# Attention in a hybrid block: the value pieces' remainders on VectorE, and seven products of the second row block ahead of the last value products

## The chip, the core and the metric

The kernel runs on one core of a Trainium2 chip. TensorE multiplies matrices into PSUM, which has 8 banks of 128 x 512 f32. VectorE (DVE in the profile), ScalarE (ACT) and GpSimd (POOL) do the rest, and SyncE (SP) issues most transfers. Each engine runs its own program in order, and the programs are tied together by semaphores: `then_inc` raises one, `wait_ge` holds an engine until it has reached a value. The metric is the time of one execution on the device in microseconds (us), median over several runs.

## The reference, cut to what matters

A block with two branches over 1024 tokens and 1024 channels: a gated delta rule and, beside it, sparse attention over latent keys and values with 8 heads of 128. Both are projected, gated and merged:

```python
ckv = rms_norm(ckv, kv_norm_g[l])
q_lat = jnp.einsum('bthd,chd->bthc', qb, w_uk[l]) * DSA_DH ** -0.5
o_lat = dsa_attention(q_lat, ckv, qi, ki, wi, rel_bias)    # softmax over the chosen keys, times the values
ob = jnp.einsum('bthc,chd->bthd', o_lat, w_uv[l]).reshape(B, T, DSA_W) * jax.nn.silu(zb)
yb = ob @ w_o_dsa[l]
out = (ga * ya + gb * yb) @ w_out[l]
x = x + gate[:, None] * out
return rms_norm(x, final_g)
```

In the kernel's words: the keys and values of each head are the latents times `w_uk` and `w_uv` ("pieces"); logits, softmax and value products follow for each head; the result `ob` times `w_o_dsa` is the projection of the merge; it is gated by `gb` and added to the half `m1` that the other branch has left in memory; and the sum `m` times `w_out` is the output. Every product is made of three f16 or bf16 products of high and low parts (`three`), so that it comes near f32.

## The kernel before, in words

Three stages stand one after the other on TensorE, each written out by hand: the delta rule, attention (`phase_attention`) and merge (`phase_merge`). The change is in attention and in the first lines of the merge.

**Attention.** There are 64 steps n, 8 for each head, in the order of tiles `ORDER = (0, 7, 1, 6, 2, 5, 3, 4)`: the step of tile i has i + 1 blocks of 128 keys. Two steps make a pair q (32 pairs), and every engine walks over the pairs.

- TensorE in pair q: `logits` of the steps 2q and 2q + 1, then `values` of the pair q - 3, then one `piece` (a half of the keys or of the values of the next head: 6 products of 512 columns or 24 of 128), then one `cut`.
- VectorE in pair q: `norm` (a reciprocal) of the pair before, two `peak` (logits plus bias, and their maximum), `gate` of pair q - 4, and `low` twice (the low part of the probabilities of the pair before).
- ScalarE in pair q: `high` twice (the high part of the probabilities of the pair before), `soften` twice (the exponentials), `piece` (the high part of the piece, out of PSUM), and `rest`.
- SyncE turns each step's probabilities with a DMA transpose (L2433) once `high` and `low` are done. `values` waits for it.
- GpSimd splits the gated result of a pair into high and low parts and raises `b_l` (L2677).

A piece m is number j = m % 4 of its head: j = 0 and 1 are keys, 2 and 3 are values. Its low part (its remainder) is what is left when the high part is taken away. For the pieces 4 to 31, TensorE does that in PSUM with one more product of 512 columns, by minus the identity (`cut`, L2482 for keys, L2484 for values), and ScalarE then copies the remainder out (`rest`, L2558 and L2560). For the pieces 0 to 3, VectorE subtracts (L2598, L2601). Pieces stand in the banks 5 and 7 by turns, and each is read by the engines one pair after it was made.

**The end of attention.** When the logits are through (pairs 32 to 34), `begin_projection` puts 4, 5 and 5 products of the merge's first two blocks (`project_rows`, three matmuls of 512 columns each) ahead of the value products of the last three pairs.

**The merge.** `project_blocks` makes 16 blocks of 8 products (k = 0 to 7). Of the first four, two have had their first seven products in `begin_projection`, one gets them at the head of `project_blocks`, ahead of the wait for `b_l` at 32, and the fourth (b, half) = (1, 1) makes all eight behind it. SyncE starts the merge's loads only when attention is over, and so do the others (`attention_left`):

```python
def attention_left(engine):
    engine.wait_ge(g.b_l, NT * H // 2)
    engine.wait_ge(g.pv, NT * H // 2)
```

In this order SyncE then loads two parts of `w_out` (L2192), two tiles of x, two rows spread over all partitions, and the first tile of `gb` (`channel_gates`, L2204). VectorE treats the 16 blocks n in order: L2298 multiplies block n by its `gb`, L2301 adds `m1`, ScalarE makes the high part `m_hi` (L2270), and L2304 makes the low part and raises `lo_ok`. GpSimd meanwhile splits six parts of weights (L2235 and L2237); the third raises `w_ready` to 3, for which TensorE waits ahead of block 8. The output products of the first tile take up k in order, and each k waits for two more low parts:

```python
if i == 0 and c0 == 0:
    pe.wait_ge(lo_ok, 2 * k + 1)
```

So k = 7 waits for the fifteenth L2304.

## Time and profile before

| | |
|---|---|
| median of 3 runs | 1370.96 us (1369.11 to 1371.2) |
| profiled execution, its own time | 1369.57 us |
| its span, first to last instruction | 1367.8 us |
| TensorE busy | 1334.2 us, 98% |
| VectorE busy | 912.9 us, 67% |
| ScalarE busy | 718.5 us, 53% |
| GpSimd busy | 593.7 us, 43% |
| attention on TensorE | about 1046 to 1202.9 us |
| the merge's projection on TensorE | 1202.9 to 1276.7 us |
| output products | 1276.7 to 1359.8 us |

The shares are averages over the whole span. TensorE's weight loads (PEld) run beside its matmuls. A matmul's duration reaches from its start to its last result, so that matmuls overlap: what one of them costs is read from the distance of two starts. Times in the trace count from the start of the span.

### The profile page before, as it was taken

How to read it: one execution, taken by the hardware profiler on the slowest of the kernel's cores; microseconds unless marked ns; L12 is line 12 of the kernel's file. 1: busy time of each engine (PE TensorE's matmuls, PEld its weight loads, DVE VectorE, ACT ScalarE, POOL GpSimd, SP SyncE). 2: the span in 40 equal slices, each digit the busy share in tenths (PEclk: the TensorE clock that was granted, in tenths of full speed). 3: DMA queues.
4: the chain of work that ended last, by engine and by line, in shares of the span. 5: the costliest groups of instructions: out<-in, count | busy, mean ns of one | idle time of the engine just before them, and what ended most of it. 6: DMA issues, size and time to landing. Idle time of an engine off the chain costs nothing.

```text
span 1367.8 us, 26191 instructions
## 1 busy us (share of the span) xinstructions
PE 1334.2 (98%) x9966; PEld 803.1 (59%) x9974; DVE 912.9 (67%) x1857; ACT 718.5 (53%) x1490; POOL 593.7 (43%) x653
## 2 busy tenths in 40 slices
PE   6899999999999999999999999999999999999997
PEld 6456994444444456666666666655445777644444
DVE  4889787777432577688788786545733788737544
ACT  4768777786443645556656645333123888701111
POOL 0074677878772434424434423002121688765000
PEclk9999999999999999999999999999999999999999
DMA  9401333333324222323233233335875988985222
GB/s 367 154 9 32 110 95 115 124 109 124 115 71 140 75 79 63 89 64 77 70 98 79 75 98 101 110 104 162 301 253 170 150 162 163 163 275 173 82 92 93
DMA packets 230056, 170.55 MB, mean 125 GB/s; under 512 B 109122, under 2 KB 202154, under 8 KB 228268
## 3 DMA queue, kind: packets, MB, share of 16 engines
q1 hardware_dynamic: 229084, 164.39, 42.7%
q10 hardware_dynamic: 720, 4.46, 0.8%
q8 instruction: 79, 1.29, 0.4%
q14 instruction: 45, 0.37, 0.1%
q0 software_dynamic: 128, 0.03, 0.0%
HBM read 114.40 MB, written 31.15 MB: 106 GB/s over the span
## 4 chain that ended last, share of the span: by engine, by line
PE 54%; POOL 4%; DVE 3%; DMA 3%; issue 2%; ACT 1%; SPq 1%; DVEq 0%; POOLq 0%; ACTq 0%
PE ps L94 15%; PE ps L96 14%; PE ps L95 14%; POOL g_shared L1434 2%; POOL g_shared L1432 1%; DVE g_yq L1674 1%; DMA g_shared<-diagonal_blocks 1%; PE ps L2065 1%; PE ps L1954 1%; DMA g_o<-g_piece 1%; PE ps L2049 1%; PE ps L2044 1%; PE ps L2048 1%; SPq L1321 1%; PE ps L2064 1%
## 5 line engine op out<-in xcount | busy, mean ns | idle before, releaser
L94 PE MATMUL ps<-g_h_hi,g_piece_hi 128*128 128x512 f16 x544 | 207.1, 381 | 1.6 <-PEq L2717 1.6
L95 PE MATMUL ps<-g_h_lo,g_piece_hi 128*128 128x512 f16 x544 | 206.5, 380 | 0.0
L96 PE MATMUL ps<-g_h_hi,g_piece_lo 128*128 128x512 f16 x544 | 206.5, 380 | 0.0
L1432 POOL TENSOR_TENSOR g_shared<-g_shared 128x120 f32<-128x120 f32 (+14 forms) x120 | 56.2, 468 | 174.5 <-DMA g_shared<-diagonal_blocks 164.2
L1042 DVE TENSOR_SCALAR_CACHE_REDUCE a_ada<-a_ada,a_s_all 128x896 bf16<-128x896 f32 (+1 forms) x124 | 113.0, 967 | 1.0
L1674 DVE SCALAR_TENSOR_TENSOR g_yq<-e_raw,g_taps,g_yq 128x1024 f32<-128x1024 f32 x60 | 96.4, 1606 | 22.1 <-ACT g_yq L1496 20.1
L94 PE MATMUL ps<-g_o,g_h_hi 128*128 128x128 f16 (+2 forms) x424 | 100.2, 267 | 3.4 <-DMA g_o<-g_piece 2.7
L96 PE MATMUL ps<-g_o,g_h_lo 128*128 128x128 f16 (+2 forms) x424 | 100.1, 267 | 0.4
L95 PE MATMUL ps<-g_o,g_h_hi 128*128 128x128 f16 (+2 forms) x416 | 97.1, 265 | 0.0
L96 PEld LDWEIGHTS ps<-g_h_hi,g_piece_lo 128*128 128x128 bf16 x544 | 53.2, 98 | 64.3 <-issue 0.2
L94 PEld LDWEIGHTS ps<-g_h_hi,g_piece_hi 128*128 128x128 f16 x544 | 53.3, 98 | 54.4 <-issue 2.0
L95 PEld LDWEIGHTS ps<-g_h_lo,g_piece_hi 128*128 128x128 f16 x544 | 53.3, 98 | 51.3
L1528 ACT ACTIVATE g_shared<-ps,e_s_neg 128x128 f32<-128x128 f32 x56 | 20.6, 367 | 100.4 <-PE ps L2049 100.1
L1434 POOL TENSOR_TENSOR g_shared<-g_shared 128x120 f32<-128x120 f32 (+14 forms) x120 | 59.9, 499 | 9.4
L310 POOL TENSOR_TENSOR a_work<-a_w,a_work 128x512 bf16<-128x512 f32 x48 | 56.5, 1193 | 15.3 <-ACT a_work L738 15.3
L310 POOL TENSOR_TENSOR a_parts<-a_w,a_parts 128x512 bf16<-128x512 f32 x48 | 55.0, 1159 | 13.3 <-ACT a_parts L738 13.3
L1665 DVE TENSOR_TENSOR g_piece_lo<-g_piece,g_piece_hi 128x1024 bf16<-128x1024 f32 x32 | 40.3, 1260 | 27.0 <-ACT g_piece_hi L1583 24.2
L755 ACT ACTIVATE a_ada<-a_ada,a_s_all 128x1024 bf16<-128x1024 f32 (+1 forms) x62 | 57.3, 927 | 0.7 <-DVEq L1064 0.7
L94 PEld LDWEIGHTS ps<-g_o,g_h_hi 128*128 128x128 f16 x424 | 41.4, 98 | 20.7 <-DMA g_o<-g_piece 3.4
L2270 ACT ACTIVATE g_h_hi<-g_arena 128x512 f32 x16 | 10.1, 630 | 80.1 <-DVE g_arena L2301 80.1
L95 PEld LDWEIGHTS ps<-g_o,g_h_hi 128*128 128x128 f16 x424 | 41.5, 98 | 16.1
L2565 ACT ACTIVATE g_o<-g_o,l_top 128x128 f32<-128x128 f32 (+3 forms) x64 | 49.0, 768 | 2.5 <-DVE l_top L2611 2.5
(450 smaller groups left out, 3983.2 us busy)
## 6 DMA issues: line engine op xcount, KB each, us to landing
a_w<-in_w_in SPq DMA_DIRECT2D x17, 1024.0 KB, 6.1
g_piece<-in_w_in SPq DMA_DIRECT2D x34, 512.0 KB, 4.2
channel_gates<-a_ada SPq DMA_DIRECT2D x48, 256.0 KB, 2.2
g_shared<-diagonal_blocks SPq DMA_DIRECT2D x32, 256.0 KB
a_ada<-in_w_ada ACTq DMA_DIRECT2D x4, 1024.0 KB, 9.8
a_x<-in_x SPq DMA_DIRECT2D x8, 512.0 KB, 9.1
delta_gate<-a_ada SPq DMA_DIRECT2D x16, 256.0 KB, 2.6
g_shared<-sums_by_head SPq DMA_DIRECT2D x8, 512.0 KB, 4.1
```

Of the source, the lines that this page charges most:

```text
L94: pe.matmul(out, a_hi, b_hi, start=first, stop=False)
L95: pe.matmul(out, a_hi, b_lo, start=False, stop=False)
L96: return pe.matmul(out, a_lo, b_hi, start=False, stop=last)
L310: nc.gpsimd.tensor_tensor(op_lo[v % 2][:, x], of, op_hi[v % 2][:, x], ALU.subtract).then_inc(w_ready, 1)
L755: nc.scalar.activation(mask[:, g.first[i]:g.first[i + 1]], score[:, g.first[i]:g.first[i + 1]], ACT.Sign, bias=trial[:, 4 + e:5 + e], accu ...
L1042: mark(("count", e), nc.vector.tensor_scalar(spent_of(i), rows_of(i), trial[:, e:e + 1], offset[:, e:e + 1], ALU.is_ge, ALU.add, accum_out ...
L1432: nc.gpsimd.tensor_tensor(part, table[:, j, :, j + 1:BASE], tc[:, :, j:j + 1].broadcast_to([P, NT, left]), ALU.mult).then_inc(sub, 1)
L1434: last = nc.gpsimd.tensor_tensor(tc[:, :, j + 1:BASE], tc[:, :, j + 1:BASE], part, ALU.subtract)
L1528: nc.scalar.activation(n_sb[:, c], at(6 + c, 1), ACT.Copy, scale=(s_neg if i else s_pos)[:, i, h:h + 1]).then_inc(n_ok[c], 1)
L1665: nc.vector.tensor_tensor(w_lo[:, m % 3], w32[:], w_hi[:, m % 3], ALU.subtract).then_inc(w_ready, 1)
L1674: nc.vector.scalar_tensor_tensor(out=y, in0=raw[:, m % 2, PAD - 3 + j:PAD - 3 + j + T], scalar=g.taps[:, tap:tap + 1], in1=y, op0=ALU.mult ...
L2565: nc.scalar.activation(p(n), p(n), ACT.Exp, scale=-1.0, bias=cell(top, n), accum_out=cell(total, n)).then_inc(exp_ok, 1)
```

## The change

The remainder of the value pieces 6, 7, 10, 11, ..., 31 (14 of them) is made by VectorE's `piece`, a subtraction out of PSUM, between `gate` and the two `low`; the 14 value products of `cut` and the 14 value copies of `rest` are gone. The key pieces keep both. `begin_projection` now makes seven more products, of the block (b, half) = (1, 0): three in its second part, ahead of the value products of the steps 60 and 61, and four in its third, ahead of those of 62 and 63. The seven products at the head of `project_blocks` are now those of block (1, 1).

```diff
@@ -2136,14 +2136,14 @@
 
 
     for k in range(KD - 1):
-        project_rows(nc, g, 0, 1, 0, k)
+        project_rows(nc, g, 0, 1, 1, k)
     pe.wait_ge(g.b_l, NT * H // 2)
     for t in range(2):
         for s in range(2):
             pe.wait_ge(w_ready, t * 2 + s + 1)
             for b in range(2):
                 for half in range(HALVES):
-                    begun = t == s == 0 and (b, half) != (1, 1)
+                    begun = t == s == 0
                     pe.wait_ge(free, t * 8 + 4 * s + 2 * b + half + 1)
                     for k in range(KD - 1 if begun else 0, KD):
                         last = project_rows(nc, g, s, b, half, k)
@@ -2406,6 +2406,10 @@
 
             return q + 4 if 0 <= q < PAIRS - 4 else None
 
+        def is_cut(m):
+
+            return m is not None and m % 4 < 2
+
         def piece_bank(m):
 
             return (0, 1, 3, 4)[m] if m < 4 else (5, 7)[m % 2]
@@ -2473,16 +2477,12 @@
                 last.then_inc(kv, 1)
 
             def cut(m):
-
                 h, j = divmod(m, 4)
                 pe.wait_ge(kv_h, m + 1)
                 if m == 4:
                     pe.wait_ge(less_ok, 1)
-                if j < 2:
-                    last = nc.tensor.matmul(bank(piece_bank(m)), less[:], k_hi[:, h % 2, j * BANK:(j + 1) * BANK], start=False, stop=True, skip_group_check=True)
-                else:
-                    last = nc.tensor.matmul(bank(piece_bank(m)), less[:], v_hi[:, h % 2, 4 * (j - 2):4 * (j - 1)], start=False, stop=True, skip_group_check=True)
-                last.then_inc(cut_ok, 1)
+                nc.tensor.matmul(bank(piece_bank(m)), less[:], k_hi[:, h % 2, j * BANK:(j + 1) * BANK],
+                                 start=False, stop=True, skip_group_check=True).then_inc(cut_ok, 1)
 
             def logits(n):
                 h, i = steps[n]
@@ -2520,6 +2520,10 @@
                     pe.wait_ge(g.w_ready, 1)
                 for k, half in [(k, half) for k in range(KD - 1) for half in range(HALVES)][(0, 4, 9)[part]:(4, 9, 14)[part]]:
                     project_rows(nc, g, 0, 0, half, k)
+                if part == 1:
+                    pe.wait_ge(top_ok, N)
+                for k in ((), (0, 1, 2), (3, 4, 5, 6))[part]:
+                    project_rows(nc, g, 0, 1, 0, k)
 
             for m in range(4):
                 piece(m)
@@ -2534,7 +2538,7 @@
                         values(n)
                 if piece_of(q) is not None:
                     piece(piece_of(q))
-                if piece_of(q - 1) is not None:
+                if is_cut(piece_of(q - 1)):
                     cut(piece_of(q - 1))
 
         @block.scalar
@@ -2552,13 +2556,9 @@
 
             def rest(m):
                 h, j = divmod(m, 4)
-                act.wait_ge(cut_ok, m - 3)
+                act.wait_ge(cut_ok, 2 * (h - 1) + j + 1)
                 act.wait_ge(kv_l, m)
-                if j < 2:
-                    nc.scalar.copy(k_lo[:, h % 2, j * BANK:(j + 1) * BANK], bank(piece_bank(m))).then_inc(kv_l, 1)
-                else:
-                    nc.scalar.copy(v_lo[:, h % 2, 4 * (j - 2):4 * (j - 1)],
-                                   bank(piece_bank(m)).rearrange("p (i d) -> p i d", d=P)).then_inc(kv_l, 1)
+                nc.scalar.copy(k_lo[:, h % 2, j * BANK:(j + 1) * BANK], bank(piece_bank(m))).then_inc(kv_l, 1)
 
             def soften(n):
                 act.wait_ge(top_ok, n + 1)
@@ -2583,7 +2583,7 @@
                     soften(2 * q + 1)
                 if piece_of(q) is not None:
                     piece(piece_of(q))
-                if piece_of(q - 1) is not None:
+                if is_cut(piece_of(q - 1)):
                     rest(piece_of(q - 1))
 
         @block.vector
@@ -2593,6 +2593,8 @@
             def piece(m):
                 h, j = divmod(m, 4)
                 dve.wait_ge(kv_h, m + 1)
+                if m >= 4:
+                    dve.wait_ge(kv_l, m)
                 if j < 2:
                     cols = slice(j * BANK, (j + 1) * BANK)
                     nc.vector.tensor_tensor(k_lo[:, h % 2, cols], bank(piece_bank(m)), k_hi[:, h % 2, cols], ALU.subtract).then_inc(kv_l, 1)
@@ -2641,6 +2643,8 @@
                     peak(2 * q + 1)
                 if q >= 4:
                     gate(q - 4)
+                if piece_of(q - 1) is not None and not is_cut(piece_of(q - 1)):
+                    piece(piece_of(q - 1))
                 if 0 <= q - 1 < PAIRS:
                     low(2 * (q - 1))
                     low(2 * (q - 1) + 1)
```

TensorE's program at the end of pair 3, the first with a value piece to cut. The names are the tiles: `g_arena` holds latents and their weights, `g_h_hi` the pieces' high parts, `g_flip_h` minus the identity.

```order
 L95 MATMUL ps<-g_arena 128x512
 L96 MATMUL ps<-g_arena 128x512
-L2484 MATMUL ps<-g_h_hi,g_flip_h 128x512
 L94 MATMUL ps<-g_h_hi,g_yq 128x256
 L95 MATMUL ps<-g_h_lo,g_yq 128x256
```

The product by minus the identity stood between a piece and the next pair's logits; now the logits follow the piece at once. The same is so at all 14 places.

VectorE's program in the last pair with a value piece (pair 28, piece 31), before:

```order
L2611 ISA g_o,l_top<-ps,g_h_hi 128x1024
L2611 ISA l_top 128x1
L2632 TENSOR_TENSOR l_b<-ps,g_o 128x256
L2622 SCALAR_TENSOR_TENSOR g_piece_lo<-g_o,l_share,g_piece_lo 128x512
L2622 SCALAR_TENSOR_TENSOR g_piece_hi<-g_o,l_share,g_piece_hi 128x640
L2618 RECIPROCAL l_share<-l_total 128x2
```

and now:

```order
L2613 ISA l_top 128x1
L2634 TENSOR_TENSOR l_b<-ps,g_o 128x256
L2603 TENSOR_TENSOR g_h_lo<-ps,g_h_hi 128x512
L2624 SCALAR_TENSOR_TENSOR g_piece_lo<-g_o,l_share,g_piece_lo 128x512
L2624 SCALAR_TENSOR_TENSOR g_piece_hi<-g_o,l_share,g_piece_hi 128x640
L2620 RECIPROCAL l_share<-l_total 128x2
```

The subtraction L2603 has come in ahead of the two `low` (L2622 before, L2624 now), and so ahead of the transposes that wait for them.

TensorE's program behind the last value product (the last row with `g_o`), where the merge begins:

```order
 L96 MATMUL ps<-g_o,g_h_lo 128x128
 L2242 UNCONDITIONAL_BRANCH
-L94 MATMUL ps<-g_yq,g_shared 128x512
-L95 MATMUL ps<-g_yq,g_shared 128x512
-L96 MATMUL ps<-g_yq,g_shared 128x512
-L94 MATMUL ps<-g_yq,g_shared 128x512
-L95 MATMUL ps<-g_yq,g_shared 128x512
-L96 MATMUL ps<-g_yq,g_shared 128x512
```

Of the rows taken away here there are 21 in all. They have moved to the front of the last value products of two pairs: 9 and 12 rows there. What follows the branch is as long as it was less these 21, so the last value product now stands 21 matmuls later in TensorE's program than before, less 14.

## Rows read from the trace of the kernel before

**Rows 1.** The page, part 1: busy time, share of the span, instructions.

```profile
PE 1334.2 (98%) x9966; PEld 803.1 (59%) x9974; DVE 912.9 (67%) x1857; ACT 718.5 (53%) x1490; POOL 593.7 (43%) x653
```

**Rows 2.** Windows: stretch, length; busy us by engine; clock, DMA share, GB/s.

```profile
1117.60:1135.60 18.00, 18.00 (x208) 13.53 (x209) 14.37 (x32) 15.99 (x33) 15.12 (x19) 1.00 0.86 164
...
1171.60:1202.90 31.30, 29.29 (x322) 20.86 (x320) 19.43 (x43) 17.46 (x34) 18.21 (x24) 1.00 0.80 146
...
1240.00:1280.00 40.00, 39.95 (x186) 18.12 (x186) 28.99 (x34) 7.28 (x12) 10.70 (x3) 1.00 0.45 146
```

**Rows 3.** Waits of PE in attention, 1045 to 1205: total us, times, longest.

```profile
PE ps L94 <- DMA g_o<-g_piece: 2.7, 3, 1.3
...
PE ps L94 <- DMA g_o<-g_piece_hi: 0.6, 1, 0.6
```

**Rows 4.** Timeline of PE at one cut: start, duration, what, [idle before].

```profile
1066.02 0.38 PE L2484 MATMUL ps<-g_h_hi,g_flip_h 128*128 128x512 f16 x1
...
1066.24 0.22 PE L94 MATMUL ps<-g_h_hi,g_yq 128*128 128x128 f16 x1
```

**Rows 5.** Sources L2484, L2560, L2601: shortest, median, longest ns, first and last start.

```profile
L2484 PE MATMUL ps<-g_h_hi,g_flip_h x14: 378/380/380, 1066.0 to 1177.5; 128*128 128x512 f16 x14
...
L2560 ACT CAST g_h_lo<-ps x14: 563/592/592, 1066.7 to 1178.6; 128x512 f16<-128x512 f32 x14
...
L2601 DVE TENSOR_TENSOR g_h_lo<-ps,g_h_hi x2: 692/692/692, 1049.6 to 1051.0; 128x512 f16<-128x512 f32 x2
```

**Rows 6.** Timeline of DVE, ACT and PE near the end of attention.

```profile
1174.90 0.29 DVE L2611 CUSTOM_DVE_ANT_0 g_o<-ps,g_arena 128x128 f32<-128x128 f32 x1 [0.39 <-PE ps L96]
...
1176.20 1.23 DVE L2611 CUSTOM_DVE_ANT_0 g_o<-ps,g_h_hi 128x1024 f32<-128x1024 f32 x1 [1.00 <-PE ps L96]
...
1179.36 0.40 DVE L2611 CUSTOM_DVE_ANT_0 g_o<-ps,g_arena 128x256 f32<-128x256 f32 x1
...
1181.29 1.41 DVE L2622 SCALAR_TENSOR_TENSOR g_piece<-g_o,l_share,g_piece 128x1024 f16<-128x1024 f32 x1
...
1180.07 1.15 ACT L2571 ACTIVATE g_piece<-g_o,l_share 128x1024 f16<-128x1024 f32 x1 [0.20 <-DMA g_o<-g_piece]
...
1187.14 0.23 PE L94 MATMUL ps<-g_o,g_h_hi 128*128 128x128 f16 x1 [1.19 <-DMA g_o<-g_piece]
```

**Rows 7.** Timeline of PE behind the last value product.

```profile
1202.89 0.38 PE L94 MATMUL ps<-g_yq,g_shared 128*128 128x512 f16 x1
...
1207.43 0.38 PE L94 MATMUL ps<-g_yq,g_shared 128*128 128x512 f16 x1
```

**Rows 8.** Timeline of POOL, SP's queue and DVE where the merge begins.

```profile
1204.06 0.67 POOL L2677 TENSOR_TENSOR g_yq<-l_b,g_yq 128x256 f16<-128x256 f32 x1
...
1204.76 1.02 SPq L2192 DMA_DIRECT2D g_shared<-in_w_out  x2
...
1218.90 0.69 DVE L2298 TENSOR_TENSOR g_arena<-ps,g_arena 128x512 f32<-128x512 f32 x1 [15.38 <-DMA g_arena<-channel_gates]
```

**Rows 9.** Timeline of DVE, PEld and PE at the first output tile.

```profile
1227.78 3.55 DVE L2304 SCALAR_TENSOR_TENSOR g_h_lo<-g_arena,g_h_hi 128x512 f32 x1 [0.93 <-ACT g_h_hi L2270]
...
1280.44 0.69 DVE L2304 SCALAR_TENSOR_TENSOR g_h_lo<-g_arena,g_h_hi 128x512 f32 x1 [0.93 <-ACT g_h_hi L2270]
...
1281.19 0.10 PEld L94 LDWEIGHTS ps<-g_o,g_h_hi 128*128 128x128 f16 x1 [0.28 <-DVE g_h_lo L2304]
...
1281.24 0.38 PE L94 MATMUL ps<-g_o,g_h_hi 128*128 128x512 f16 x1
```

**Rows 10.** Timeline of POOL and PE where block 8 begins.

```profile
1226.38 4.39 POOL L2237 TENSOR_TENSOR g_shared<-g_shared 128x2048 bf16<-128x2048 f32 x1
...
1235.27 0.38 PE L94 MATMUL ps<-g_yq,g_shared 128*128 128x512 f16 x1
```

**Rows 11.** Timeline of PE, and a window, where the granted clock fell.

```profile
536.66 0.36 PE L2008 MATMUL ps<-g_arena,g_shared 64*64 64x32 f32 x5 [1.93 <-DVE g_shared L1846]
...
538.00:541.50 3.50, 3.50 (x18) 3.19 (x18) 2.66 (x13) 3.48 (x5) 0.00 (x0) 0.51 0.02 5
```

## The prediction, made before the changed kernel had run

> **What bounds the kernel now.** I read the page first: TensorE is busy 98% of the span [rows 1]. A share over the whole span could hide a stage with another limit, so I went on to the windows of one head of attention, of its end, and of the merge. In a head TensorE is busy 18.00 of 18.00 us, with the transfers at 0.86 of their engines, VectorE at 14.4 us and ScalarE at 16.0; in the last 31.3 us of attention it lacks 2.0 us; in the merge it lacks 0.05 us of 40 [rows 2]. Then the waits of TensorE in attention: all that it waits for there are DMA transposes, 3.3 us in four waits [rows 3]. So in the middle and in the merge a matmul less is time won, and at the end of attention it is not. Last I read the timelines around each place that the change touches, for the slack of those who are waited for. That is where this change is decided, and it is not in attention.
>
> **What the change takes away: 14 products on TensorE.** One `cut` occupies TensorE from 1066.02 to 1066.24, 0.22 us [rows 4]; from a longer stretch of such matmuls, the 21 from 1202.89 to 1207.43, one is 0.216 us [rows 7]. Fourteen of them [rows 5] are 3.0 us. The 14 copies of 0.59 us on ScalarE [rows 5], 8.3 us, lie beside TensorE's work; their going costs and brings nothing by itself.
>
> **What it adds: 14 subtractions on VectorE.** The same operation on the same tile took 0.69 us in the first four pieces [rows 5]. It stands behind the second `peak` of its pair and ahead of the two `low`, so it delays that pair's transposes and the next `norm` and `peak`. In the middle of attention VectorE waits for TensorE in each pair: 0.39 us ahead of one peak and 1.00 ahead of the next in the pair shown [rows 6], and a head has 3.6 us of such time (18.0 less 14.4 [rows 2]) for two subtractions, 1.4 us. So there I cost it at nothing; its cover is VectorE's idle time. With that cover gone a head costs 1.4 less the 0.43 that it won. The transposes that TensorE waited for belong mostly to the tiles of 1024 keys [rows 3, 6], whose `low` come one pair after the value pieces, when the delay has been absorbed by that idle time.
>
> At the end that cover is gone. From the peak at 1176.20 on VectorE runs without a wait: `peak` at 1179.36, `low` at 1181.29 [rows 6]. There is no piece left to make, TensorE needs less than VectorE for a pair, and it stands still until 1187.14 for the transpose of that `low` [rows 6]. Piece 31 is subtracted inside this run. That peak has 13 cuts ahead of it, so it comes 13 x 0.216 = 2.8 us earlier; the `low` behind it 2.8 - 0.7 = 2.1. ScalarE waits there 0.20 us for an older transpose [rows 6], which has itself been delayed by piece 30; I take 2.0. The fourteenth cut is then lost in the wait. **So TensorE reaches its last value product 2.0 us earlier by this half of the change.** Bounds: 3.0 (nothing of it is lost) and 1.0 (two further transposes arrive late by half a subtraction or more; in rows 3 there are already waits of this kind).
>
> **What it moves: seven products, 21 matmuls, 4.54 us** from 1202.89 to 1207.43 [rows 7]. They leave the place behind the last value product and stand in front of it. TensorE's sum doesn't change: seven other products fill the old place, and these are missing from block (1, 1) further on. They cover there the wait for `b_l` as before: the last split on GpSimd ended at 1204.73, 1.8 us behind the last value product, well inside 4.5 us [rows 7, 8]. The two waits for transposes at the end (1.19 and 0.6 us) lie ahead of the moved products and don't shrink by them.
>
> But everything that the merge needs from others starts with the end of attention. SyncE's first load went out at 1204.76, at once behind that split; the first `gb` tile had landed and VectorE began its 16 blocks at 1218.90, after 15.38 us of waiting [rows 8]. No load of this sequence was held by TensorE. Against TensorE's count of matmuls the whole sequence now starts 4.54 us later. Which of its ends is late next?
>
> - `w_ready` 3: GpSimd ended the split at 1226.38 + 4.39 = 1230.77; TensorE began block 8 at 1235.27 [rows 10]. Slack 4.50 us against 4.54: gone, but hardly overdrawn, some 0.1 us.
> - `lo_ok` 15: VectorE ended the fifteenth `low` part at 1280.44 + 0.69 = 1281.13. TensorE's weight load for k = 7 waited 0.28 us for it and went at 1281.19, the matmul followed without a gap at 1281.24 [rows 9]. Slack 0.05 us.
>
> The second is the one. TensorE had made the sixteenth block at 1276.7, before VectorE was through with its fifteenth, so VectorE doesn't wait for it there, and its last result moves with its start. From the end of the last split, 1204.73, to that `low` part are 76.4 us that no engine but SyncE, GpSimd, VectorE and ScalarE takes part in. Hence TensorE, which comes to k = 7 2.0 us earlier than before, stands still there for 4.54 - 0.05 = 4.5 us (with the 0.1 us of `w_ready` inside it), and the end of the kernel moves by 4.5 - 2.0 = **+2.5 us**. Behind it the output products are bound by TensorE again, and nothing gives the time back.
>
> **The clock behind a standstill.** The only fall of the granted clock inside the work came 1.3 us after a wait of 1.93 us at 536.66, ran from 538.0 to 541.5 at 0.51, that is at 1.2 in place of 2.4 GHz [rows 11], and so cost half of 3.5 us, 1.75, had all of it been matmuls. A wait of 1.19 us at 1187.14 was followed by none (clock 1.00 in that window) [rows 2, 6]. The new standstill is longer than both. I put its cost between 0 and 1.75 us and take 0.85, since the fall needs a moment that may or may not come while TensorE works. The Trainium skill, in "TensorE: Matmul & The Clock Gate", in the table of practical rules, warns of idle gaps between bursts of matmuls, since they bring the array back to half clock. By that rule the fall is sure, and the sum would be 0.9 us higher than with my middle value; by the row alone it is open.
>
> **The sum.** -2.0 + 4.5 + 0.85 = +3.35 us. On the profiled execution's own time, 1369.57, that makes 1372.9. That execution was 1.4 us faster than the median, 1370.96, which is what the result will be: 1370.96 + 3.35 = **1374.3 us**, +0.24%.
>
> **The rivals.**
>
> 1. *VectorE becomes the bound in the value pairs.* For it: in the window of a head DVE and DMA are at 0.80 and 0.86 [rows 2], and a transpose that leaves 0.7 us later meets full queues. Against: VectorE's waits before both peaks. Then the 3.0 us are eaten up and the stall stays: +4.5 + 0.85 = +5.3, 1376.3.
> 2. *The stall doesn't come, and the kernel is faster.* VectorE's way through the 16 blocks isn't rigid: a `low` part took 3.55 us at 1227.78 and 0.69 at 1280.44 [rows 9], longer while GpSimd splits weights. The four or five such operations hold some 14 us. If the new position against GpSimd and the transfers saved more than 4.5 us of it, TensorE would find its operands ready and the gain of 2.0 would stand: 1369.0. From 2.5 us saved on it is no longer slower than before. Against: GpSimd's splits start from the same loads, so both move together.
> 3. *Part of that*: 1 to 2.5 us of the chain are won back, and no clock falls: 0 to +1.5, 1371.0 to 1372.5.
> 4. *The clock falls fully* behind the stall: k = 7 and the 24 matmuls of the second half run at 1.2 GHz for 3.5 us. +2.5 + 1.75 = +4.25, 1375.2. It differs from my forecast in that term alone and lies in its range. The clock page of the Trainium skill, named above, speaks for it.
>
> **How the numbers follow.** The forecast, a stall of 4 to 5 us at k = 7 with a gain of 1.2 to 2.6 ahead of it and 0 to 1.75 for the clock, has 0.63 (of it 0.3 for rival 4); rival 1 has 0.12; rival 2 0.12; rival 3 0.13. The forecast's own range is 1.9 to 5.1: 1372.9 to 1376.1. For 8 in 10 I take in rival 3 and the lower half of rival 1 and leave out rival 2: 1371.0 to 1377.0. A measurement of this kernel can tell about 0.2%, 2.7 us, from no change. Slower by more than that: the forecast's cases with a clock that falls or a gain under 1.8 us (0.44) and rival 1 (0.12): 0.56. Within it: the rest of the forecast (0.19), rival 3 and most of rival 2: 0.37, since 2.0 us won is itself under that bound. Faster by more: 0.07.
>
> **What the profile after would show.** L2484 and L2560 gone, 14 more subtractions of 0.69 us; TensorE waiting at the last two tiles of 896 and 1024 keys somewhat longer than 1.2 and 0.6 us; the last value product near 1202.9 + 4.5 - 2.0 = 1205.4, SyncE's first `w_out` load near 1207.3 and the first L2298 near 1221.4; a wait of TensorE for `w_ready` of 0.1 us at most at block 8; and at k = 7 of the first output tile a gap of 4.4 us that ends with L2304, at about 1283.7, perhaps with the clock at 0.5 behind it. I would be wrong if VectorE's stretch from SyncE's first load to the fifteenth L2304 were not 76.4 us, or if TensorE waited for more transposes in the middle of attention.

## The result, and the profile after

| | before | after |
|---|---|---|
| median of 6 runs | 1369.76 us (1367.99 to 1371.20) | 1376.78 us (1373.32 to 1378.42) |
| ratio, 95% interval | | 1.0051 (1.0038 to 1.0063) |
| profiled execution, its own time | 1369.57 us | 1376.63 us |
| its span | 1367.8 us | 1374.6 us |
| TensorE busy | 1334.2 us | 1335.2 us |

The changed kernel is 7.0 us slower (5.2 to 8.6). The forecast was 1374.3, 3.35 us slower: the direction and the stall were as foreseen, and the forecast difference was half of the measured one. The median of the kernel before is 1369.76 here; the forecast started from 1370.96, the median of three of these six runs.

The page of the changed kernel, part 1, answers to [rows 1]:

```profile
PE 1335.2 (97%) x9960; PEld 803.4 (58%) x9960; DVE 925.0 (67%) x1871; ACT 711.8 (52%) x1476; POOL 595.3 (43%) x653
```

VectorE has 14 instructions more and 12.1 us more: 13.6 more in attention, 1.5 less elsewhere. Fourteen subtractions of 0.69 us are only 9.7. ScalarE has 14 fewer. TensorE should have lost 3.0 us and shows 1.0 more; the two falls of its clock described below add some 1.7 us each.

The waits of PE from 1045 to 1295 in the changed kernel (total us, times, longest), to be read beside [rows 3] and the 0.28 of [rows 9]:

```profile
PE ps L94 <- DVE g_h_lo L2304: 4.2, 1, 4.2
PE ps L94 <- DMA g_o<-g_piece: 4.1, 4, 2.0
PE ps L94 <- DMA g_o<-g_piece_hi: 1.6, 4, 0.6
...
PE ps L94 <- DVE l_top L2613: 1.1, 1, 1.1
```

The first is the foreseen stall. The other three, all in attention, make 6.8 us where there were 3.3: 3.5 more, and one of them, for `peak` (`l_top`), is of a kind that didn't exist before. (Left out is a wait of 1.1 us for ScalarE's copy of a key piece, L2558 before and L2561 now, the same in both. So the prediction's "all that it waits for there are DMA transposes" was not quite right, but the change doesn't touch that wait.)

By place, the 3.5 us are 0.7 in the wait for the first transposes, 1.4 in the middle and 1.3 in the last pairs. In the middle, between 1090 and 1175, the kernel before has no wait at all. The changed kernel there:

```profile
PE ps L94 <- DMA g_o<-g_piece: 0.9, 2, 0.6
PE ps L94 <- DMA g_o<-g_piece_hi: 0.5, 2, 0.3
```

**Attention.** PE of the changed kernel: the first product of attention, the new wait for `peak`, and the first product behind the last value product.

```profile
1042.67 0.38 PE L94 MATMUL ps<-g_arena 128*128 128x512 f16 x1
...
1181.55 0.39 PE L94 MATMUL ps<-g_h_hi,g_yq 128*128 128x512 f16 x1 [1.09 <-DVE l_top L2613]
...
1208.06 0.38 PE L94 MATMUL ps<-g_yq,g_shared 128*128 128x512 f16 x1
```

From the first row to the last are 165.38 us; the same two products stood at 1044.90 and 1202.89 [rows 7] before, 157.99 apart. Of the 7.39 us more, 4.54 are the moved matmuls. About 1.7 are a fall of the clock, which ran at 0.57 behind a transpose wait of 2.0 us near 1060; the trace before has none there. Windows of the changed kernel, columns as in [rows 2]: that fall, the stall, the fall behind the stall, and one head.

```profile
1062.00:1066.00 4.00, 4.00 (x46) 4.00 (x44) 1.25 (x3) 2.31 (x5) 0.00 (x0) 0.57 0.45 99
...
1282.00:1286.30 4.30, 0.18 (x1) 0.00 (x0) 2.66 (x5) 1.15 (x2) 0.00 (x0) 1.00 0.00 0
1287.60:1291.10 3.50, 3.50 (x11) 1.24 (x10) 0.74 (x2) 0.63 (x1) 0.00 (x0) 0.55 0.00 0
...
1117.80:1135.80 18.00, 18.00 (x218) 13.78 (x216) 16.06 (x35) 15.45 (x32) 14.77 (x19) 1.00 0.82 165
```

The rest, 1.15 us, is the value half of the change (0.45) and a wait for the first transposes that was 0.7 us longer. I don't count that wait to the change: the transpose that it waits for is issued at 1055.67, ahead of the first of the new subtractions at 1060.85, and among the eleven profiled executions it lies between 1.3 and 2.0 us, at 1.4 and 1.5 also in two with the value half (experiments 9 and 7). So the 3.0 us that the 14 `cut` gave back were all lost again, and a little more. In the head above, VectorE is busy 16.06 us where it was 14.37 [rows 2]: 1.7 us for two subtractions that I had down for 1.4.

The `low` parts show where the excess is. DVE's groups in the changed kernel, 1040 to 1205 (count | busy us, mean ns | idle before), first the three shapes of `low`, then the `peak` of the large tiles:

```profile
L2624 DVE SCALAR_TENSOR_TENSOR g_piece_hi<-g_o,l_share,g_piece_hi 128x128 f16<-128x128 f32 (+3 forms) x32 | 31.1, 973 | 2.4 <-ACT g_piece_hi L2571 2.4
L2624 DVE SCALAR_TENSOR_TENSOR g_piece<-g_o,l_share,g_piece 128x1024 f16<-128x1024 f32 (+1 forms) x16 | 22.1, 1381 | 0.8 <-ACT g_piece L2571 0.8
...
L2624 DVE SCALAR_TENSOR_TENSOR g_piece_lo<-g_o,l_share,g_piece_lo 128x256 f16<-128x256 f32 (+1 forms) x16 | 12.6, 785 | 0.4 <-ACT g_piece_lo L2571 0.4
...
L2613 DVE CUSTOM_DVE_ANT_0 g_o<-ps,g_h_hi 128x1024 f32<-128x1024 f32 (+1 forms) x16 | 18.4, 1152 | 3.1 <-PE ps L96 3.1
```

The 64 `low` take 31.1 + 22.1 + 12.6 = 65.8 us; the same groups before gave 27.3 + 21.1 + 10.2 = 58.6. (7.2 and 9.7 are more than the 13.6 of attention, since each of these instructions starts some 0.08 us before the one ahead of it ends, and a few other groups are shorter.) And the idle time ahead of the large `peak`, which was to be the cover, has shrunk from 11.2 us to 3.1.

One pair in the timelines of the changed kernel, DVE and then POOL, at the last value piece:

```profile
1175.53 1.22 DVE L2613 CUSTOM_DVE_ANT_0 g_o<-ps,g_h_hi 128x1024 f32<-128x1024 f32 x1 [0.36 <-PE ps L96]
...
1177.02 0.68 DVE L2603 TENSOR_TENSOR g_h_lo<-ps,g_h_hi 128x512 f16<-128x512 f32 x1
1177.62 1.24 DVE L2624 SCALAR_TENSOR_TENSOR g_piece_lo<-g_o,l_share,g_piece_lo 128x512 f16<-128x512 f32 x1
1178.79 1.29 DVE L2624 SCALAR_TENSOR_TENSOR g_piece_hi<-g_o,l_share,g_piece_hi 128x640 f16<-128x640 f32 x1
```

```profile
1177.17 0.40 POOL L2679 CAST g_yq<-l_b 128x256 f16<-128x256 f32 x1 [1.73 <-DVE l_b L2634]
1177.64 0.67 POOL L2681 TENSOR_TENSOR g_yq<-l_b,g_yq 128x256 f16<-128x256 f32 x1
1178.27 1.12 POOL L2667 TENSOR_TENSOR g_arena<-g_arena 128x256 f32<-128x256 bf16 x1
```

In the same pair before the change the two `low` took 0.74 and 1.02 us, and GpSimd's cast and split, which `gate` releases, 0.85 and 1.13. DVE and POOL of the kernel before:

```profile
1177.68 0.74 DVE L2622 SCALAR_TENSOR_TENSOR g_piece_lo<-g_o,l_share,g_piece_lo 128x512 f16<-128x512 f32 x1
1178.34 1.02 DVE L2622 SCALAR_TENSOR_TENSOR g_piece_hi<-g_o,l_share,g_piece_hi 128x640 f16<-128x640 f32 x1
...
1177.83 0.85 POOL L2675 CAST g_yq<-l_b 128x256 f16<-128x256 f32 x1 [1.60 <-DVE l_b L2632]
1178.76 1.13 POOL L2677 TENSOR_TENSOR g_yq<-l_b,g_yq 128x256 f16<-128x256 f32 x1
```

Now the `low` take 1.24 and 1.29, the cast and the split 0.40 and 0.67. With the subtraction between `gate` and `low`, GpSimd is at work first, and the delay has changed sides: from GpSimd, where it is free, to VectorE. The Trainium skill, "SBUF — State Buffer", section "Who interferes with whom", says that a VectorE instruction with two SBUF inputs contends with a GpSimd one that reads SBUF, and that the order of issue decides which of them is held. The trace agrees where it can tell: before the change `low` began first (1177.68, the cast at 1177.83) and the cast was the longer, now the cast begins first (1177.17, `low` at 1177.62) and keeps its 0.40. The split and the `low` beside it begin within 0.02 us of each other (`low` at 1177.62, the split at 1177.64), and it is `low` that is the longer, so for that pair the trace doesn't show the order deciding.

**Merge.** SyncE's queue, DVE and PE in the changed kernel, answering to [rows 8] and [rows 9]:

```profile
1209.92 1.02 SPq L2192 DMA_DIRECT2D g_shared<-in_w_out  x2
```

```profile
1224.08 0.69 DVE L2298 TENSOR_TENSOR g_arena<-ps,g_arena 128x512 f32<-128x512 f32 x1 [15.40 <-DMA g_arena<-channel_gates]
...
1285.62 0.69 DVE L2304 SCALAR_TENSOR_TENSOR g_h_lo<-g_arena,g_h_hi 128x512 f32 x1 [0.93 <-ACT g_h_hi L2270]
```

```profile
1281.81 0.38 PE L96 MATMUL ps<-g_o,g_h_lo 128*128 128x512 f16 x1
...
1286.38 0.39 PE L94 MATMUL ps<-g_o,g_h_hi 128*128 128x512 f16 x1 [4.19 <-DVE g_h_lo L2304]
```

From SyncE's first load to the end of the fifteenth `low` part are 76.40 us, before 76.38 (1204.76 to 1281.13). The chain kept its length, as forecast. At k = 7 TensorE waits 4.19 us; from start to start are 4.57 us, 4.36 more than a matmul takes. Behind it the clock ran at 0.55 for 3.4 us (third window above), and from that `low` part to the end of the span are 88.3 us in place of 86.6: the fall cost 1.65.

### The profile page after: what moved, and what is told of

Read it like the earlier page. It is cut to its first block, busy times and chain, and to the rows that moved or that the text cites. A ratio compares the mean times of both kernels' runs of the same rounds, so it can differ in the third digit from the quotient of the medians.

```text
span 1374.6 us, 26171 instructions
## 1 busy us (share of the span) xinstructions
PE 1335.2 (97%) x9960; PEld 803.4 (58%) x9960; DVE 925.0 (67%) x1871; ACT 711.8 (52%) x1476; POOL 595.3 (43%) x653
## 3 DMA queue, kind: packets, MB, share of 16 engines
q8 instruction: 79, 1.29, 0.4%
## 4 chain that ended last, share of the span: by engine, by line
PE 52%; DVE 5%; DMA 3%; issue 3%; POOL 2%; ACT 2%; SPq 0%; DVEq 0%; ACTq 0%; POOLq 0%
PE ps L94 14%; PE ps L96 13%; PE ps L95 13%; DMA g_o<-g_piece_hi 1%; POOL g_shared L1432 1%; PE ps L2065 1%; DVE g_yq L1674 1%; POOL g_shared L1434 1%; DMA g_o<-g_piece 1%; PE ps L2049 1%; PE ps L2044 1%; PE ps L2048 1%; PE ps L1954 1%; PE ps L2064 1%; DVE g_arena L2301 1%
## 5 line engine op out<-in xcount | busy, mean ns | idle before, releaser
L94 PE MATMUL ps<-g_o,g_h_hi 128*128 128x128 f16 (+2 forms) x424 | 101.8, 269 | 9.9 <-DVE g_h_lo L2304 4.2
L95 PE MATMUL ps<-g_o,g_h_hi 128*128 128x128 f16 (+2 forms) x424 | 101.8, 269 | 0.0
L1665 DVE TENSOR_TENSOR g_piece_lo<-g_piece,g_piece_hi 128x1024 bf16<-128x1024 f32 x32 | 40.3, 1259 | 27.1 <-ACT g_piece_hi L1583 24.3
L2270 ACT ACTIVATE g_h_hi<-g_arena 128x512 f32 x16 | 10.1, 629 | 84.6 <-DVE g_arena L2301 84.6
L96 PEld LDWEIGHTS ps<-g_o,g_h_lo 128*128 128x128 f16 x424 | 41.9, 99 | 14.7 <-issue 0.7
```

Of the source, the lines that this page charges most:

```text
L94: pe.matmul(out, a_hi, b_hi, start=first, stop=False)
L95: pe.matmul(out, a_hi, b_lo, start=False, stop=False)
L96: return pe.matmul(out, a_lo, b_hi, start=False, stop=last)
L1665: nc.vector.tensor_tensor(w_lo[:, m % 3], w32[:], w_hi[:, m % 3], ALU.subtract).then_inc(w_ready, 1)
```

## The experiments

Each was run five rounds beside the kernel before; "attention" is the distance of the two products named above, 157.99 us before the change, in the profiled execution.

**1. The value half alone.** The diff of the change without its lines on products:

```diff
-                if piece_of(q - 1) is not None:
+                if is_cut(piece_of(q - 1)):
                     cut(piece_of(q - 1))
...
+                if piece_of(q - 1) is not None and not is_cut(piece_of(q - 1)):
+                    piece(piece_of(q - 1))
                 if 0 <= q - 1 < PAIRS:
                     low(2 * (q - 1))
```

> The value pieces' remainders on VectorE, as in the change, and the projection's products where they were before. The reason given in the prediction (a subtraction is hidden in VectorE's idle time until the last pairs) expects attention 2.0 us shorter and the kernel 2.0 us faster than before. The rival after the result (the subtraction delays both low parts and pushes them onto GpSimd's split, where they take longer) expects attention about 1.2 us longer, that is 7.4 us longer in the changed kernel's trace less 4.54 for the moved products and 1.7 for a fall of the clock; the kernel 1 to 2 us slower. Both expect no wait of TensorE at k = 7 of the first output tile beyond the 0.05 us of slack.

Measured: 1371.22 against 1369.1, ratio 1.0017 (1.0005 to 1.0028), attention 159.81. The half that was to bring 2.0 us costs 2.3 (0.7 to 3.8). Waits of PE in its attention:

```profile
PE ps L94 <- DMA g_o<-g_piece: 4.8, 4, 2.0
PE ps L94 <- DMA g_o<-g_piece_hi: 1.8, 4, 0.7
...
PE ps L94 <- DVE l_top L2609: 1.1, 1, 1.1
```

They make 7.7 us, 4.4 more than before, against 3.0 won: +1.4, and attention measures +1.8. Of that, 0.7 is again the wait for the first transposes, which leaves 1.1 for the value half. In the middle of attention TensorE waits 2.1 us for transposes, and at k = 7 it waits 0.3 us.

**2. The seven products alone.**

```diff
-        project_rows(nc, g, 0, 1, 0, k)
+        project_rows(nc, g, 0, 1, 1, k)
...
+                for k in ((), (0, 1, 2), (3, 4, 5, 6))[part]:
+                    project_rows(nc, g, 0, 1, 0, k)
```

> Only the seven products moved; the value pieces are cut on TensorE as before. The chain theory expects the last value product 4.5 us later, 76.4 us from SyncE's first load to the fifteenth L2304 as before, a standstill of 4.4 us at k = 7 and a fall of the clock behind it: 4.5 + 1.5 = 6 us slower, 4.5 if the clock holds. The rival that the chain's end isn't what stops TensorE (the change's loss is all in attention) expects no change.

Measured: 1376.32 against 1369.1, ratio 1.0059 (1.0044 to 1.0074), attention 162.64, 4.65 more. Timeline of PE and a window:

```profile
1284.38 0.61 PE L94 MATMUL ps<-g_o,g_h_hi 128*128 128x512 f16 x1 [4.43 <-DVE g_h_lo L2304]
```

```profile
1284.00:1287.50 3.50, 3.12 (x8) 1.19 (x9) 2.31 (x4) 0.63 (x1) 0.00 (x0) 0.51 0.02 5
```

The stall and the fall of the clock are there without the value half: 4.65 in attention, 0.2 in the chain (76.54 us) and 1.5 for the clock make 6.3 us in the profile, 8.1 (6.0 to 10.1) timed, where the medians are 7.2 apart. The moved products carry nearly all of the loss. The two halves don't add up exactly (2.3 and 8.1 against 7.0), which their intervals allow.

**3. The change, with SyncE's merge loads released early.** The weights' and `gb`'s loads no longer wait for the end of attention, only for the events that free the memory they go to:

```diff
-            attention_left(sp)
+            sp.wait_ge(g.kv, 4 * H)
+            sp.wait_ge(g.near_ok, 3 + NT - 2 + NT * H)
+            sp.wait_ge(w_ready, 2)
```

> The changed kernel, but SyncE starts the merge's loads when the pieces, the masks and the weight splits that share their memory are through, not when the last gate is; behind the last transpose it is free at about 1197, 11 us ahead of the last value product. The chain theory expects the first gb tile landed by the time that VectorE is done with the last gate, VectorE's chain some 7 us earlier against TensorE, no standstill at k = 7 and no fall of the clock there: 5 to 6 us faster than the changed kernel, 1 us slower than before or as fast. The rival (transfers of the merge collide with the last transposes, and the standstill moves to those) expects less than 2 us of it.

Measured: 1370.38 against 1369.1, ratio 1.0011 (1.0002 to 1.0020): 1.5 us slower than before, so that 5.5 us of the 7 are gone. SyncE's queue and DVE:

```profile
1199.98 1.07 SPq L2194 DMA_DIRECT2D g_shared<-in_w_out  x2
```

```profile
1216.18 0.69 DVE L2300 TENSOR_TENSOR g_arena<-ps,g_arena 128x512 f32<-128x512 f32 x1 [4.87 <-PE ps L96]
```

The first load goes out 10.7 us ahead of TensorE's last value product. VectorE now waits for TensorE's first block and not for `gb`; the fifteenth `low` part ended at 1281.21, TensorE, which came to k = 7 at 1284.51, had no wait from 1211 to the end, and the clock did not fall there. The rival's collision didn't come. So the stall goes when the loads alone start earlier. What stays is the loss inside attention, 165.97, with a fall of the clock near 1064: less 4.54 for the moved products, 1.7 for that fall and 0.7 for the first wait, the value half costs 1.1 us in this trace, as in experiment 1.

**4. The value half, with the subtraction behind both `low`.** The other half as before the change.

```diff
-                if piece_of(q - 1) is not None and not is_cut(piece_of(q - 1)):
-                    piece(piece_of(q - 1))
                 if 0 <= q - 1 < PAIRS:
                     low(2 * (q - 1))
                     low(2 * (q - 1) + 1)
+                if piece_of(q - 1) is not None and not is_cut(piece_of(q - 1)):
+                    piece(piece_of(q - 1))
```

> The value pieces' remainders on VectorE, but behind the two low parts of the pair; products as before. If the loss in attention comes from low parts that are late and that run against GpSimd's split, the low parts go back to their durations and places of before (0.61, 1.15, 0.74 and 1.02 us in the value pairs) and attention gains: 14 cuts, 3.0 us, less 0.7 in the last pairs, so 2 us faster than before. If it is VectorE's total work that is too much, it is no faster than with the value part as in the change.

Measured: 1367.44 against 1369.1, ratio 0.9988 (0.9976 to 1.0000), attention 156.38. DVE at the last value piece:

```profile
1176.30 0.74 DVE L2620 SCALAR_TENSOR_TENSOR g_piece_lo<-g_o,l_share,g_piece_lo 128x512 f16<-128x512 f32 x1
1176.96 1.02 DVE L2620 SCALAR_TENSOR_TENSOR g_piece_hi<-g_o,l_share,g_piece_hi 128x640 f16<-128x640 f32 x1
1177.90 0.68 DVE L2599 TENSOR_TENSOR g_h_lo<-ps,g_h_hi 128x512 f16<-128x512 f32 x1
```

The same 14 subtractions, elsewhere in VectorE's program: both `low` have their old durations, and attention is 3.4 us shorter than in experiment 1 (156.38 against 159.81), the timed median 3.8 us. In the middle of attention TensorE waits 0.2 us for transposes where it waited 2.1. VectorE's idle time ahead of the large `peak` shrinks here too, from 11.2 to 4.9 us, and does no harm. The gain of the 14 `cut` is real; the place of the subtraction took it.

**5. The value half, with the subtraction ahead of `gate`.** This keeps the delay of the `low` and takes away the meeting with GpSimd.

```diff
+                if piece_of(q - 1) is not None and not is_cut(piece_of(q - 1)):
+                    piece(piece_of(q - 1))
                 if q >= 4:
                     gate(q - 4)
```

> Value part only, with the subtraction ahead of gate in VectorE's pair, products as before. gate, which starts GpSimd's split, is then as late as the low parts, so that these stand against GpSimd as before the change, and only their delay of 0.6 us is left. If contention with GpSimd is a cost of its own, the low parts of 384, 768, 512 and 640 keys go back from 0.8, 1.4, 1.1 and 1.2 us to 0.73, 1.15, 0.79 and 1.0, and attention is 0.5 to 1.5 us shorter than with the value part alone as in the change (159.8 us). If delay is all that matters, attention is as long as there or longer.

Measured: 1370.33 against 1369.0, ratio 1.0010 (0.9999 to 1.0021), attention 158.85. Two rows of DVE:

```profile
1173.86 0.74 DVE L2620 SCALAR_TENSOR_TENSOR g_piece_lo<-g_o,l_share,g_piece_lo 128x512 f16<-128x512 f32 x1
1174.52 1.02 DVE L2620 SCALAR_TENSOR_TENSOR g_piece_hi<-g_o,l_share,g_piece_hi 128x640 f16<-128x640 f32 x1
```

`low` is short again, and so are all 64: 27.1 + 21.2 + 10.7 = 59.0 us in the groups that had 58.6 before the change and 65.8 behind it. Yet attention gains only 1.0 us on experiment 1, while experiment 4 gains 3.4. So the meeting with GpSimd looks like the smaller part, 1.0, and the lateness of what follows the subtraction like the larger, 2.5. The times of experiments 1 and 5 don't tell the two apart; this split rests on the profiled executions, of which there is one for each. Nor did the 1.0 us reach the end of the kernel. The chain from SyncE's first load to the fifteenth `low` part was 78.0 us long in this execution, and TensorE waited at k = 7:

```profile
1279.41 0.39 PE L94 MATMUL ps<-g_o,g_h_hi 128*128 128x512 f16 x1 [1.38 <-DVE g_h_lo L2304]
```

In the ten profiled executions in which the loads start behind attention, the chain is between 76.3 and 78.0 us long; why it was longest here no run shows.

**6. The kernel before, with `begin_projection` one pair earlier.** Its products then stand ahead of the value products that TensorE waited for longest, and fill those waits.

```diff
-                if q >= PAIRS:
-                    begin_projection(q - PAIRS)
+                if PAIRS - 1 <= q < PAIRS + 2:
+                    begin_projection(q - PAIRS + 1)
```

> The kernel before, with the 4, 5 and 5 products of begin_projection ahead of the value products of the pairs 28, 29 and 30 in place of 29, 30 and 31. TensorE waits for transposes ahead of the value products of steps 57 and 59, 1.2 and 0.6 us, and no product stood in front of the first. If products ahead of the last value products help only where they fill such a wait, these two waits go, the last value product comes 1.8 us earlier, SyncE's first load with it, and nothing stops TensorE at k = 7: 1.8 us faster than before. The rival (the waits move on to the steps 61 to 63, which now have no product in front of them) expects no change.

Measured: 1367.55 against 1369.0, ratio 0.9983 (0.9971 to 0.9996), attention 156.17. TensorE's waits for transposes are 1.7 us in place of 3.3; the two of 1.2 and 0.6 us are gone, and none came in their place. At k = 7 it waits 0.5 us.

**7. Experiments 4 and 6 together.**

```diff
+                if PAIRS - 1 <= q < PAIRS + 2:
+                    begin_projection(q - PAIRS + 1)
...
                     low(2 * (q - 1) + 1)
+                if piece_of(q - 1) is not None and not is_cut(piece_of(q - 1)):
+                    piece(piece_of(q - 1))
```

> Value part with the subtraction behind the low parts, and begin_projection one pair earlier. The first took 1.6 us from attention, the waits for transposes that were left at its end were 1.9 and 0.5 us, and these are what the second fills: the last value product 3.5 to 4 us earlier than before, 3.5 us faster than before. The rival (VectorE is the bound of the last pairs whatever stands on TensorE) expects no more than the better one of the two alone, 1.7 us.

Measured: 1366.04 against 1369.0, ratio 0.9977 (0.9964 to 0.9989), attention 153.72. It is 3.1 us faster than the kernel before (1.5 to 4.9) and, since the changed one is 7.0 us slower, some 10 us faster than that. Waits of PE in attention:

```profile
PE ps L94 <- DMA g_o<-g_piece: 1.5, 1, 1.5
...
PE ps L94 <- DMA g_o<-g_piece_hi: 0.5, 1, 0.5
PE ps L94 <- DVE l_top L2609: 0.3, 1, 0.3
```

**8. Experiment 7, with the pieces 30 and 31 cut on TensorE again.**

```diff
-            return m is not None and m % 4 < 2
+            return m is not None and (m % 4 < 2 or m >= 30)
```

> As the version with the subtraction behind the low parts and begin_projection one pair earlier, but the last two value pieces (30 and 31) are cut on TensorE and copied by ScalarE as before the change. Their subtractions stand where VectorE has no idle time. If that costs more than the two cuts (0.43 us), attention is up to 1 us shorter than 153.7 us and TensorE's wait for a peak at the pair 29 (0.3 us) goes; the rival (behind the low parts a subtraction delays nothing that TensorE waits for) expects 0.4 us longer. Either way within what the timing can tell; the trace decides.

Measured: 1367.74 against 1370.33, ratio 0.9980 (0.9967 to 0.9992), attention 155.26, 1.5 us longer than in experiment 7 (0.5 of it in the first wait). The wait for `peak` went, but nothing was gained by it. By time the two can't be told apart, and the trace speaks for the rival: with the subtraction behind `low`, the last two do no harm on VectorE.

**9. Experiment 1, with the pieces 30 and 31 cut on TensorE again.** The same edit of `is_cut`, on the value half as in the change.

```diff
-            return m is not None and m % 4 < 2
+            return m is not None and (m % 4 < 2 or m >= 30)
```

> The value part alone as in the change, but pieces 30 and 31 as before the change. The prediction put all of this part's loss into the last pairs: then attention goes from 159.8 to 156 us or less, with two of fourteen cuts back. If the loss is spread over the heads, since low parts are late and long in each value pair, about 1 to 1.5 us of it goes and attention stays above 158 us, longer than before the change (158.0).

Measured: 1370.60 against 1370.33, ratio 1.0003 (0.9994 to 1.0012), attention 157.44. The wait for `peak` is gone, and those for transposes are 4.6 us, where experiment 1 had 6.6. Attention is 2.4 us shorter than in experiment 1; 0.65 of that lies in the wait for the first transposes, far ahead of these pieces, so that two of 14 pieces carry 1.7. The other twelve should have won 2.6 against the kernel before and won 0.55: they lose ahead of the end as well. The result lies between the two expectations, neither of which was met: the last two pieces carry more than the "1 to 1.5 us" of the one and less than the 3.8 us of the other.

## Why the prediction was right in direction and half the size

**How near it came.** The measured median, 1376.78, lies above the forecast's own range, which ended at 1376.1, and just inside the one for 8 in 10, which ended at 1377.0. That it lies inside is partly luck: the forecast counted from 1370.96, and the kernel before has its median at 1369.76 over six runs. The difference of 7.0 us is more than the 6.0 that the range left above the old median.

**Right: the stall.** The step "TensorE ... stands still there for 4.54 - 0.05 = 4.5 us" held: 4.4 us by starts, at the same instruction, behind a chain of 76.40 us where 76.4 was said. Experiment 2 makes it by itself and experiment 3 removes it by releasing the loads. `w_ready` held block 8 for 0.14 us, where 0.1 was said. So rivals 2 and 3 were wrong: none of the chain was won back. SyncE's first load, the first L2298 and the end of the stall stood at their foreseen distances from the last value product, which itself came at 1208.0 and not at 1205.4, in an execution that reached attention 2.2 us earlier.

**Right: the 14 cuts themselves,** 3.0 us. With the subtraction behind `low` the half brought 1.6 us of time (0.0 to 3.3, experiment 4).

**Wrong: "So there I cost it at nothing; its cover is VectorE's idle time."** This is the step that failed, and with it "So TensorE reaches its last value product 2.0 us earlier by this half of the change". In place of -2.0 us the half measured +2.3 us (0.7 to 3.8) in experiment 1. In the traces, with the long first wait and the clock taken out, it is +1.1 in experiments 1 and 3 and +0.45 in the changed kernel. The last pairs cost nearly what was said: 1.3 us more waiting, against the 1.0 that the prediction took off its 3.0. What had been put at nothing is the middle, where TensorE waits 1.4 us for transposes in the changed kernel and 2.1 in experiment 1, against none before. The prediction had named more waits for transposes there as a sign that it was wrong. Another 0.6 to 0.7 us lies in gaps of TensorE too short for the list of waits. Idle time ahead of the *peak* was real (11.2 us, now 3.1), but it is no cover for the *low* directly behind the subtraction: those two start later by the whole subtraction whether or not VectorE rests afterwards, and so do the transposes that wait for them. I let the delay be absorbed one pair later. Experiments 4 and 9 show that it was not, in the last two pieces (where a new wait of 1.1 us for `peak` came) and in the earlier ones. That TensorE waits for just the transposes that left late is read from the order of the program; no experiment moved them one by one.

**Missed: the order of `gate` and `low`.** The diff put an instruction between them, and I didn't ask what `gate` releases. GpSimd's cast and split then ran ahead of `low` and held it: 7 us more in 64 `low`, worth about 1 us of attention in the trace (experiment 5 against 1). Rival 1, with a chance of 0.12, said that the 3.0 us would be eaten up and the stall stay, and with 1376.3 came nearest to the time. Its argument that transposes leave later held. That VectorE becomes the bound did not: in the head shown it is busy 16.1 of 18.0 us, and experiment 4 has the same subtractions without the loss.

**Sized at half: the clock behind the stall.** I took 0.85 between 0 and 1.75. It fell behind the stall in both profiled kernels that had it, and cost 1.65 and 1.5 us. The Trainium skill's rule on idle gaps in "TensorE: Matmul & The Clock Gate", named in the prediction, agrees with both stalls, and I should have counted nearly all of the 1.75.

**The sum again, with what was measured:** +4.4 for the stall and 1.65 for the clock behind it come to +6.05. The value half adds 0.45 in the trace of the changed kernel, and makes +6.5 against +7.0 timed; with the 1.1 of experiments 1 and 3 it would be 7.2. By either, of the 3.65 us that the forecast lacked some 2.5 to 3.1 are the value half and 0.8 the clock. In the one profiled span, +6.8, the rest cancels: 1.7 for the fall near 1062 and 0.7 for the first wait against 2.2 us by which that execution reached attention earlier, where nothing was changed. (Up to 1.7 of those 2.2 are the fall near 538 of [rows 11], which the changed kernel's trace doesn't have.) What stays open is how much of the 7.0 is the fall near 1062. Of eleven traces two have it, this one and that of experiment 3, which can't say how often it comes. Nor was it tried what the change gives with the subtraction behind `low` and the early loads together.

## What to carry to other kernels

Work moved ahead of the last event that releases the next stage's loads delays the whole stage; look for the chain behind that event and its slack first, here 0.05 us, and either keep the order or release the loads by what they really need. Idle time on an engine covers a new instruction only if it lies between that instruction and the first result that someone waits for: put the new one behind that result, which made 3.4 us of difference here with the same work. Where an inserted instruction comes between one that releases GpSimd and one on VectorE that reads two operands from SBUF, ask which of the two engines will be at work first.

## What the runs showed of the hardware

- In one pair `low` on 128x512 took 0.74 us before and 1.24 after the change, and on 128x640 1.02 and 1.29, where GpSimd's cast of 128x256 began 0.15 us behind the first of them and 0.45 us ahead of it. The cast took 0.85 and 0.40, the split 1.13 and 0.67, the other way round.
- The clock fell for 3.4 us behind both stalls of 4.2 and 4.4 us, and also behind transpose waits of 2.0 us near 1060 in two traces (the changed kernel and experiment 3), but not behind waits as long at the same place in experiments 1, 5 and 8 (2.0 us each). The length of the wait alone does not tell it.
- Attention began between 1040.7 and 1046.1 us in eleven executions of kernels that are alike up to there, so that a difference of one span against another carries up to 5 us that belong to no edit. A part of it is the clock: the six traces with a fall near 538 begin attention at 1044.2 or later, the five without one at 1044.5 or earlier.
